# Paged cache compression in a one-core decoder step: page numbers read eight at once without a run-time check, and a third engine that requests pages

## The reference, cut to what matters

```python
past = kv_pages[page_table]                 # 64 pages of 128 rows for each of 8 requests
past = past.reshape((b, -1) + past.shape[3:])
...
kc, vc, cend = compress_kv(full[:, :, 0], full[:, :, 1], p)

def compress(kv, pe, w1, w2):               # once for keys, once for values
    ...
    pieces = kv[...].reshape(b, n_c + r - 1, CMP_STRIDE, NSA_KV_HEADS, HEAD_DIM)
    hid = sum(jnp.einsum('bncgd,cdf->bngf', pieces[:, p:p + n_c] + pe_r[p][:, None, :], w1_r[p]) for p in range(r))
    return jnp.einsum('bngf,fd->bngd', jax.nn.gelu(hid), w2)
```

## Time and profile before

| | us |
|---|---|
| median of 3 runs (3681.19 to 3713.42) | 3697.57 |
| the profiled execution | 3702.29 |
| its span from first to last instruction | 3700.5 |
| cache compression, from the start of the span | about 893 |
| TensorE busy in the whole span | 3057.1 (83%) |
| scalar engine busy | 1135.0 (31%) |

### The profile page before, as it was taken

The page is one execution under the profiler, slowest core; times in us unless marked ns, Lnnn a source line. Parts: engine busy times, 40 slices in busy tenths (PEclk is TensorE's granted clock), DMA queues, the critical chain, the costliest instruction groups (busy, mean ns, idle before and its releaser), DMA issues. The chain is left out here.

```text
span 3700.5 us, 50558 instructions
## 1 busy us (share of the span) xinstructions
PE 3057.1 (83%) x17167; PEld 2653.1 (72%) x17167; DVE 1507.8 (41%) x3336; ACT 1135.0 (31%) x2011; POOL 546.2 (15%) x855
## 2 busy tenths in 40 slices
PE   4699979998497657699999445899987799999996
PEld 4477757876396447577777212898876799999995
DVE  3355556554514550134556311011133444544446
ACT  3467657774321211133444000011112211111112
POOL 4344525540001000000000175000000000000000
PEclk9899989998698758777888655699998899999998
DMA  8567767771512314400000232411122211111111
GB/s 124 81 107 120 116 99 118 116 113 37 189 46 92 115 49 143 138 18 6 12 12 0 95 105 77 135 43 40 34 86 98 69 45 57 34 46 56 34 34 46
DMA packets 280169, 276.19 MB, mean 75 GB/s; under 512 B 48666, under 2 KB 237582, under 8 KB 279352
## 3 DMA queue, kind: packets, MB, share of 16 engines
q1 hardware_dynamic: 226878, 189.34, 19.8%
q0 software_dynamic: 37376, 59.36, 8.6%
q10 hardware_dynamic: 15738, 25.40, 3.5%
HBM read 241.17 MB, written 36.71 MB: 75 GB/s over the span
## 5 line engine op out<-in xcount | busy, mean ns | idle before, releaser
L237 POOL DMA_DIRECT2D raw<-in_cache_nsa_kv x640 | 382.3, 597 | 445.7 <-issue 416.0
L2186 PE MATMUL bank<-u2H,fwiH 128*128 128x344 f32 x1056 | 338.0, 320 | 39.3 <-DVE fwiL L2553 39.3
L398 ACT ACTIVATE cy<-bank 64x512 f32<-64x512 f32 x512 | 303.5, 593 | 148.5 <-PE bank L279 141.6
L2186 PE MATMUL bank<-u2H,fwiL 128*128 128x344 f32 x1056 | 337.5, 320 | 0.0
L2186 PE MATMUL bank<-u2L,fwiH 128*128 128x344 f32 x1056 | 337.4, 320 | 0.0
L2186 PE MATMUL bank<-cxH,cwH 128*128 128x512 f32 x768 | 324.8, 423 | 2.8 <-DVE cxL L510 2.8
L2186 PE MATMUL bank<-cxL,cwH 128*128 128x512 f32 x768 | 307.0, 400 | 0.0
L2186 PE MATMUL bank<-cxH,cwL 128*128 128x512 f32 x768 | 306.9, 400 | 0.0
L2186 PEld LDWEIGHTS bank<-u2H,fwiH 128*128 128x128 f32 x1056 | 199.2, 189 | 39.8 <-issue 39.8
L279 PE MATMUL bank<-ident,raw 128*128 128x128 f32 x1024 | 142.9, 285 | 72.0 <-DMA raw<-in_cache_nsa_kv 68.7
L2186 PEld LDWEIGHTS bank<-u2H,fwiL 128*128 128x128 f32 x1056 | 199.0, 188 | 0.0
(11 more groups left out here) (479 smaller groups left out, 6419.9 us busy)
## 6 DMA issues: line engine op xcount, KB each, us to landing
raw<-in_cache_nsa_kv POOLq DMA_DIRECT2D x640, 64.0 KB, 6.5
raw<-in_cache_nsa_kv SPq DMA_DIRECT2D x384, 64.0 KB
fwi<-in_w_ffn_in SPq DMA_DIRECT2D x44, 512.0 KB
wada<-in_w_ada ACTq DMA_DIRECT2D x8, 2048.0 KB
fwo<-in_w_ffn_out SPq DMA_DIRECT2D x22, 512.0 KB
gwg<-in_w_in SPq DMA_DIRECT2D x20, 512.0 KB
mwada<-in_w_ada SPq DMA_DIRECT2D x4, 2048.0 KB, 8.8
mwada<-in_w_ada_final SPq DMA_DIRECT2D x4, 2048.0 KB, 8.1
```

The source lines that it names most:

```text
L237: eng.dma_start(raw[8 * q:8 * q + 8, t % 2, nt], pages[bass.ds(at[n], 1), :, :, P * kv:P * kv + P] .rearrange("o n s c -> (o n) s c")).the ...
L398: ins = act.activation(y[HD * odd:HD * odd + HD, kk % 3, 0:2, g, 0:HP], k.bank[6 + odd][HD * g:HD * g + HD, :].rearrange("p (i r) -> p r i ...
L2186: mm = pe.matmul(out, a[x], b[y], start=start and n == 0, stop=stop and n == 2)
```

## The change

Page numbers are read eight at once, and without the check at run time. The 64 pages are eight groups of eight: GpSimd takes groups 0, 2, 3, 5 and 6 (40 pages as before, though not the same ones), SyncE groups 1 and 4 (16 pages), and the scalar engine group 7 (8 pages). The scalar engine requests its pages of images 0 and 1 at the start, behind its list of small loads and ahead of the rounding of weights. For image t+2 it requests two pages at the end of each of four rounds: j = 5, 6 and 7 of image t, and j = 0 of image t+1. TensorE waits for a third semaphore.

```diff
-        MINE = {ET.SP: [4 * nt + q for nt in range(4) for q in ((2, 3) if nt % 2 else (3,))]}
-        MINE[ET.Pool] = [q4 for q4 in range(16) if q4 not in MINE[ET.SP]]
+        MINE = {ET.SP: [1, 4], ET.Pool: [0, 2, 3, 5, 6]}
+        AQ = 7
+        def page_numbers(et, t, q8):
+            b = t % B
+            return nc.values_load_multi_w_load_instructions(
+                pt[0:1, b * NPAGES + 8 * q8:b * NPAGES + 8 * q8 + 8], engines=(et,), min_val=0, max_val=POOL - 1,
+                skip_runtime_bounds_check_because="the page table holds numbers of pages of the cache, by its meaning")[1]
+        def load_page(eng, t, q8, n, at, sem):
+            kv = t // B
+            nt, q = q8 // 2, 8 * (q8 % 2) + n
+            eng.dma_start(raw[8 * q:8 * q + 8, t % 2, nt], pages[bass.ds(at[n], 1), :, :, P * kv:P * kv + P]
+                          .rearrange("o n s c -> (o n) s c")).then_inc(sem[t % 2], 16)
...
             if t == 1:
-                eng.wait_ge(s_psp[0], 64 * len(MINE[ET.SP]))
-                eng.wait_ge(s_pool[0], 64 * len(MINE[ET.Pool]))
+                eng.wait_ge(s_psp[0], 128 * len(MINE[ET.SP]))
+                eng.wait_ge(s_pool[0], 128 * len(MINE[ET.Pool]))
...
+            for q8 in MINE[et]:
+                at = page_numbers(et, t, q8)
+                for n in range(8):
+                    load_page(eng, t, q8, n, at, sem)
...
+                        pe.wait_ge(s_pact[t % 2], 128 * (t // 2 + 1))
...
+            act.wait_ge(s_pt, 16)
+            for t in range(2):
+                at = page_numbers(ET.Activation, t, AQ)
+                for n in range(8):
+                    load_page(act, t, AQ, n, at, s_pact)
             for n in range(NJ):
                 round_w(n)
...
+                nt = (kk - 5) // NJ + 2
+                if kk >= 5 and nt < NI and (kk - 5) % NJ < 4:
+                    if j == 5:
+                        act.wait_ge(s_tr, 2 * NJ * (nt - 1))
+                        at = page_numbers(ET.Activation, nt, AQ)
+                    for n in range(2 * ((kk - 5) % NJ), 2 * ((kk - 5) % NJ) + 2):
+                        load_page(act, nt, AQ, n, at, s_pact)
                 if t and j == 5:
                     store(t - 1)
```

More of the change, by code:

```diff
@@ L191, in cache_compress @@
     s_psp, s_pool = [[k.sem(f"s_c_{x}{j}") for j in range(2)] for x in ("psp", "pool")]
+    s_pact = [k.sem(f"s_c_pact{j}") for j in range(2)]
     s_wc = [k.sem(f"s_c_wc{j}") for j in range(2)]
@@ L219, in cache_compress @@
         block = ctx.enter_context(nc.Block())
-        MINE = {ET.SP: [4 * nt + q for nt in range(4) for q in ((2, 3) if nt % 2 else (3,))]}
-        MINE[ET.Pool] = [q4 for q4 in range(16) if q4 not in MINE[ET.SP]]
+        MINE = {ET.SP: [1, 4], ET.Pool: [0, 2, 3, 5, 6]}
[10 more added lines that the diff above has]
+                          .rearrange("o n s c -> (o n) s c")).then_inc(sem[t % 2], 16)
         def load_pages(eng, et, t, sem):
-            kv, b = t // B, t % B
             if t == 1:
-                eng.wait_ge(s_psp[0], 64 * len(MINE[ET.SP]))
-                eng.wait_ge(s_pool[0], 64 * len(MINE[ET.Pool]))
+                eng.wait_ge(s_psp[0], 128 * len(MINE[ET.SP]))
+                eng.wait_ge(s_pool[0], 128 * len(MINE[ET.Pool]))
             if t >= 2:
                 eng.wait_ge(s_tr, 2 * NJ * (t - 1))
[L232 to L238, removed]
+            for q8 in MINE[et]:
+                at = page_numbers(et, t, q8)
+                for n in range(8):
+                    load_page(eng, t, q8, n, at, sem)
         def switch(t, j):
@@ L275, in turn @@
                     if j == 0 and odd == 0:
-                        pe.wait_ge(s_psp[t % 2], 64 * len(MINE[ET.SP]) * (t // 2 + 1))
-                        pe.wait_ge(s_pool[t % 2], 64 * len(MINE[ET.Pool]) * (t // 2 + 1))
+                        pe.wait_ge(s_psp[t % 2], 128 * len(MINE[ET.SP]) * (t // 2 + 1))
+                        pe.wait_ge(s_pool[t % 2], 128 * len(MINE[ET.Pool]) * (t // 2 + 1))
+                        pe.wait_ge(s_pact[t % 2], 128 * (t // 2 + 1))
                     for nt in range(4):
@@ L443, in store @@
                     act.dma_start(k.vc_d[:, b, :, :].rearrange("p t d -> p (t d)"), kc_vc[:, :]).then_inc(s_kst, 16)
+            nc.disable_value_cache = True
+            at = None
             act.dma_start(perow, k.i["cmp_pe"][0].rearrange("v (j s) d -> (v j) (s d)", s=2)).then_inc(s_pe, 16)
@@ L496, in _ @@
             store(NI - 1)
+            nc.disable_value_cache = False
         @block.vector
```

## The result

The change is slower: 3759.27 us (median of 4 runs, 3757.46 to 3770.28) against 3699.17 (4 runs, 3681.19 to 3713.42), a ratio of 1.0195 [1.0161, 1.0229]. I had forecast 3664, range 3624 to 3712.

The account below looks back on a forecast made before the run. Behind a slow front the stage was taken as TensorE's, with holes from late pages. The terms +20 - 32.5 - 2.2 - 26 - 8 + 4 + 6 = -38.7 us, from 3702.3, gave 3664, range 3624 to 3712.

Parts of the forecast that it names:

- Eight pages to the scalar engine, in the rounds: Scalar engine's two requests a round: 2.1 us, covered by 3.2 us of copies and waiting; ends 0 and 40, taken +4.
- the third rival: Scalar engine's requests held behind `wada`, delaying its rounding for TensorE; 12 us uncovered per odd image, +46, 3748 us; chance 0.10.
- Sixteen requests at the start: Scalar engine's requests ahead of the first weight chunk delay the first transpose by 12.7 to 31 us; taken +20.
- Image 1: TensorE's page wait before image 1 goes, as eight pages are requested early: -32.5 us, and 2.2 of half clock.
- The other holes: TensorE's remaining page waits, 36.2 us, shrink by three quarters: -26, and -8 for the half clock behind them.
- the rival that transfers bind: Page transfers limit, whoever requests them; late images stay late, only front and image 1 change: -4.7, 3698 us; chance 0.28.
- Checks removed: On SyncE and GpSimd, requests come earlier: SyncE's 16 pages 16.5 us unheld, GpSimd's 40 in 31; worth only what transfers allow.
- Change of weights: In image 7, page requests ahead of the weight chunk lengthen TensorE's 20.9 us wait for it: +6.
- Both signs: Forecast wrong if page waits sum to over 30 us, or TensorE waits for VectorE's remainder behind held scalar-engine requests.

Follow-up runs that it names:

- e4: The change with `wada` issued behind the eighth page request of the odd image, not ahead of the first: 3691.95 us, ratio 1.0003.
- e8: The change with `wada` from the second slice on requested by GpSimd on its own queue, ahead of its 40 pages: 3664.95 us, ratio 0.9898.
- e2: The change without the scalar engine's requests at the start; SyncE takes those pages of images 0 and 1: 3768.74 us, ratio 1.0213.
- e6: The kernel before with numbers read eight at once, unchecked (SyncE 24 pages, GpSimd 40), and `wada` loaded later: 3746.56 us, ratio 1.015.
- e7: The change with `wada` loaded later and SyncE requesting the scalar engine's pages of images 0 and 1: 3679.31 us, ratio 0.9944.
- e3: The change with SyncE requesting all 24 pages from image 2 on; the scalar engine's requests at the start stay: 3693.28 us, ratio 1.0019.
- e9: e5 without the check of page numbers, same pages on the same engines: 3702.72 us, ratio 1.0021.
- e5: The kernel before with only `wada` loaded later, between the page requests: 3662.85 us, ratio 0.9908.
- e16: e8 with the run-time check back on SyncE and GpSimd: 3685.76 us, ratio 0.9995.

## Why the prediction was wrong

**The step that failed** is "Eight pages to the scalar engine, in the rounds": "I cost the issue at nothing", **+4**. It took the issue of `wada` itself, 0.51 us, as the nearest row. That row shows the load going out, with one 256 KB chunk ahead of it. A page request beside `wada` has its nearest row elsewhere: SyncE's 17 us an image, which I had read, and spread over eight pages. The 11.2 us of the earlier trace rows, which I had taken for another, is none: that request stands in image 0, before the first `wada`, and beside `wada` SyncE's longest was 7.1:

```profile
31.51 11.24 SPq L237 DMA_DIRECT2D raw<-in_cache_nsa_kv  x1
```

So requests can also be held without `wada`, as the 16 at the start were. Nor did I count that the store stands behind the requests on the same queue; it alone was held up to 7.46 us. Had the 17 us been taken whole, less the cover, the sum was there: it is the third rival, "the scalar engine inherits the hold", at 12 us an odd image and 3748 us, to which I gave 0.10. What it says against itself, that SyncE's queue held 24 pages and this one has eight, was the wrong thing to count: the same eight requests are held with the 2 MB of `wada` ahead of them and nearly free without (e4, e8). Nor did the chunk of 0.37 us behind `wada` speak for a page request.

The size, as an estimate: the stretches from even to odd images grew by 63.8 us although three things in them shrank or left: 34.5 us of page waits (36.2 less the 1.7 before image 10), 10.4 us lost at half clock behind these, and 15.5 of the 20.9 us that TensorE waited for the chunk in the change of weights (now 5.4). That makes the held issues, with the low clock behind them, 63.8 + 34.5 + 10.4 + 15.5 = 124 us in place of +4: some 18 an odd image, where the whole hold is 22.6.

The other steps:

- *Sixteen requests at the start*, +20: measured +40.5 (100.1 against 59.6), past my long end of 31. The 16 requests took 42.9 us, 2.7 each, against the 2.2 that I took from SyncE as the held pace. SyncE's 16 requests beside them took 30.6 us, 1.9 each, so three issuers do not hold every request longer; why the scalar engine's were held longer stays open.
- *Image 1*, -32.5: right. Its transposes start 39.2 us after the first (I had 39.4), with no hole. Front and image 1 together make +8.0, not -14.7. e2 against the change shows that the pair brings nothing either way.
- *The other holes*, -26 and -8: the pages do come in time, all of them (2.0 us of waits left), and they do in e4 and e8 too (0.9 and 2.6 us), where nearly all of these holds are gone, so the rival that transfers bind is wrong for this split. The Trainium skill (DMA: Bandwidth & Descriptors, "Issuing engines are not separate DMA queues") has it that further issuers save only the sequencer's time, which it calls usually small. Here two issuers kept 95.8 us of page waits (e6) and three, all else alike, 16.8 (e7), with a ratio of 0.9944 and not 1.015: the time at the sequencer is not small where requests are held, and the measurement decides. It is not so in every setting: in e3 two issuers from image 2 on kept only 7.7. In the change itself the gain was not TensorE's, since TensorE was now late by another way.
- *Checks removed*: GpSimd's 40 pages take 29.9 us (I had 31; my 4.1 us for four of SyncE's should have read 4.2, and nothing hangs on it), SyncE's 16 are still held, 36 to 41 us on odd images from 3 on. "It moves no byte less, so it is worth only what the transfers allow" was too mild for one split and too strict for another: with 24 pages on SyncE it costs a per cent (e9 against e5), with 16 and `wada` on GpSimd's queue it brings one (e8 against e16).
- *Change of weights*, +6: image 8 to 9 took 78.0 us, was 71.0. The number is right by luck: I had the chunk later behind the pages, near 27 us, but TensorE's wait for it fell from 20.9 to 5.4 us. The scalar engine came late instead, with the 20.2 us behind held requests before `cwH`.

Both signs that I had named for a wrong forecast were to be looked for; the second came true: TensorE waits for VectorE behind held requests on the scalar engine.

## What to carry to other kernels

Price a DMA request by what is on the way when it is issued, and by a row of its own kind: beside a 2 MB load, behind two page requests, a 256 KB store took 7.46 us to issue, and right behind the load alone 0.35. A hold costs SyncE only what its pages then come late; it is dear on an engine whose next instruction feeds TensorE. Here moving the large load to GpSimd's queue freed the computing engine. And removing instructions from an engine that waits for transfers need not make the transfers quicker: here it made one kernel slower (e9) and another faster (e8).

## What the runs showed of the hardware

- A held DMA issue stops the engine's work behind it in program order: 9.68 us of idle scalar engine behind one store.
- GpSimd was not held by the same load: with `wada` ahead of them on its queue (e8), its 40 page requests of an image took 29.9 to 30.4 us on odd and even images alike. There the 2 MB landed in 12.0 us, on the scalar engine's queue in 33.5 (issue to landing, from the page of e8 and of the change):

```profile
wada<-in_w_ada POOLq DMA_DIRECT2D x7, 2048.0 KB, 12.0
```

```profile
wada<-in_w_ada ACTq DMA_DIRECT2D x8, 2048.0 KB, 33.5
```

- An issue with its address in a register mostly lasts 0.69 to 0.71 us on the scalar engine where nothing holds it (e8), a store with a fixed address 0.33 to 0.35 in the kernel before.
- Sooner is not earlier: the same 64 pages an image, requested without checks, kept TensorE waiting 111.3 us in e9's profile against 44.3 in e5's.
- A 2 MB load on the scalar engine's hardware queue goes with holds on SyncE's as well: 16 requests took 39.4 us on image 3 of the change, 23.7 in e8.
